# Strip sums S1, S2 and S4 in two PSUM banks with the products reordered, and the remainder of S3 made on GpSimd behind that of A12

## What is computed

```
def half_swiglu(x, g, w_up, w_down):
    h = rms_norm(x, g)
    a, b = jnp.split(h @ w_up, 2, axis=-1)
    return x + 0.5 * ((jax.nn.silu(a) * b) @ w_down)
```

## Time and profile before

| what | value |
|---|---|
| median of 3 runs | 2734.58 us (2734.44 to 2734.65) |
| span of the profiled execution | 2732.7 us |
| around its span, against the median of the runs | 1.9 us |
| PE busy | 2707.3 us, 99% |
| DVE busy | 1729.2 us, 63% |
| ACT busy | 1103.5 us, 40% |
| POOL busy | 999.8 us, 37% |
| mean granted TensorE clock | 0.998 |

### The profile page before, as it was taken

The page is one execution under the profiler, slowest core; times in us unless marked ns, Lnnn a source line. Parts: engine busy times, 40 slices in busy tenths (PEclk is TensorE's granted clock), DMA queues, the critical chain, the costliest instruction groups (busy, mean ns, idle before and its releaser), DMA issues. The chain is left out here.

```text
span 2732.7 us, 46951 instructions
## 1 busy us (share of the span) xinstructions
PE 2707.3 (99%) x18804; PEld 2646.4 (97%) x18804; DVE 1729.2 (63%) x2801; ACT 1103.5 (40%) x1858; POOL 999.8 (37%) x610
## 2 busy tenths in 40 slices
PE   9999999999999999999999999999999999999998
PEld 8999999998999999999999999999989999999997
DVE  8747576887433693838685647668773347837475
ACT  5324244636322352424443333454463224424242
POOL 2333333345433333333333333333544333333332
PEclk9999999999999999999999999999999999999999
DMA  3222222233122222222222222222332222222222
GB/s 118 99 71 93 77 87 93 88 124 125 63 71 91 75 73 84 78 93 78 94 77 85 70 95 78 92 86 88 132 109 70 77 88 74 75 79 78 93 78 85
DMA packets 72853, 238.04 MB, mean 87 GB/s; under 512 B 8304, under 2 KB 17264, under 8 KB 72176
## 3 DMA queue, kind: packets, MB, share of 16 engines
q1 hardware_dynamic: 57888, 208.30, 22.1%
q10 hardware_dynamic: 14800, 27.51, 2.9%
HBM read 227.52 MB, written 8.27 MB: 86 GB/s over the span
## 5 line engine op out<-in xcount | busy, mean ns | idle before, releaser
L498 POOL TENSOR_TENSOR w_lo<-w_raw,w_hi 128x1024 fp32r<-128x1024 f32 (+1 forms) x254 | 600.0, 2365 | 962.8 <-ACT w_hi L1131 947.7
L1131 ACT ACTIVATE w_hi<-w_raw 128x1024 fp32r<-128x1024 f32 (+1 forms) x238 | 250.2, 1051 | 796.1 <-PE lin L635 660.8
L635 PE MATMUL lin<-h_hi,w_hi 128*128 128x320 f32 x1600 | 373.8, 315 | 2.9 <-DVE tmp L1614 2.7
L635 PE MATMUL lin<-h_hi,w_lo 128*128 128x320 f32 x1600 | 364.6, 309 | 0.0
L635 PE MATMUL lin<-h_lo,w_hi 128*128 128x320 f32 x1600 | 364.1, 309 | 0.0
L635 PE MATMUL lin<-g_hi,w_lo 128*128 128x320 f32 x1408 | 320.9, 309 | 0.0
L635 PE MATMUL lin<-g_lo,w_hi 128*128 128x320 f32 x1408 | 320.8, 309 | 0.0
L635 PE MATMUL lin<-g_hi,w_hi 128*128 128x320 f32 x1408 | 320.7, 309 | 0.0
L550 POOL TENSOR_TENSOR lo_A<-raw_even,hi_A 128x512 fp32r<-128x512 f32 x120 | 167.8, 1398 | 376.3 <-ACT hi_A L1185 376.3
L635 PEld LDWEIGHTS lin<-h_hi,w_hi 128*128 128x128 f32 x1600 | 265.2, 188 | 15.9 <-issue 11.3
L635 PEld LDWEIGHTS lin<-h_lo,w_hi 128*128 128x128 f32 x1600 | 267.5, 188 | 0.0
(11 more groups left out here) (334 smaller groups left out, 6215.6 us busy)
## 6 DMA issues: line engine op xcount, KB each, us to landing
w_raw<-wts SPq DMA_DIRECT2D x240, 512.0 KB, 3.5
raw_even<-wts SPq DMA_DIRECT2D x88, 512.0 KB, 4.4
raw_odd<-wts SPq DMA_DIRECT2D x64, 512.0 KB, 4.2
caches<-kcache_in ACTq DMA_DIRECT2D x16, 512.0 KB, 4.0
caches<-vcache_in ACTq DMA_DIRECT2D x16, 512.0 KB, 4.7
x<-x_in SPq DMA_DIRECT2D x8, 320.0 KB, 6.6
k_out<-kT ACTq DMA_DIRECT2D x2, 1280.0 KB, 4.6
v_out<-v_sb ACTq DMA_DIRECT2D x2, 1280.0 KB, 8.6
```

Of the source, the lines that this page charges most:

```text
L498: ins = nc.gpsimd.tensor_tensor(w_lo[:, s, cols], w_raw[:, s, cols], w_hi[:, s, cols].bitcast(F), ALU.subtract)
L635: ins = nc.tensor.matmul(out[:, half, :], w, a[:, half * HALF:(half + 1) * HALF], start=first and n == 0, stop=last and n == 2)
L1131: nc.scalar.activation(w_hi[:, s, 0:cols], w_raw[:, s, 0:cols], ACT.Copy).then_inc(hi_ready.sem, 1)
```

## The change

Three things. (1) The sums S1, S2 and S4 of every pair but the first of a segment are made in place, one over the other, in a PSUM bank (`chain[i % 2]`, the two banks of `lin[1]`, which the linear tiles use outside the segments); pair 0 keeps SBUF strips. (2) M5(i) goes right behind M1(i), and the lists of ACT and DVE are written anew to fit. (3) The remainder of S3 is made by POOL, behind that of A12, for all pairs but the first of a segment.

```
+        chain = [lin[1][:, 0, :], lin[1][:, 1, :]]
...
@@ POOL, ffn
                             low_strip(L, q + i + 1, i + 1, "A12")
+                            low_strip(L, q + i + 1, i + 1, "S3")
...
@@ PE, segment
                         pe.wait_ge(evacuated.sem, evacuated.count(L, m))
+                    m5(L, q + i, i)
                     m6(L, q + i, i)
...
                     m7(L, q + i, i)
-                    m5(L, q + i, i)
                 m4(L, q + e, e)
...
@@ ACT, first_pair
                 hi_strip(L, q + 1, 1, "A11", "M1")
-                hi_strip(L, q + 1, 1, "S2", "M6")
+                hi_strip(L, q + 1, 1, "S1", "M5")
                 act.wait_ge(evacuated.sem, evacuated.count(L, m))
                 nc.scalar.activation(last_a[:, :], last_a[:, :], ACT.Silu).then_inc(silu_done.sem, 1)
                 hi_strip(L, q + 1, 1, "A12", "M2")
+                hi_strip(L, q + 1, 1, "S2", "M6")
                 hi_strip(L, q + 1, 1, "S3", "M7")
-                hi_strip(L, q + 1, 1, "S1", "M5")
...
@@ ACT, segment
                         hi_strip(L, q + i + 1, i + 1, "A11", "M1")
+                        hi_strip(L, q + i + 1, i + 1, "S1", "M5")
+                    if not i:
+                        hi_strip(L, q, 0, "A22")
+                        hi_strip(L, q, 0, "S4")
+                    if more:
+                        hi_strip(L, q + i + 1, i + 1, "S2", "M6")
                     if i:
+                        hi_strip(L, q + i, i, "A22", "M4")
+                        hi_strip(L, q + i, i, "S4", "M3")
                         silus(L, q + i - 1, i - 1)
                     if more:
                         hi_strip(L, q + i + 1, i + 1, "A12", "M2")
-                        hi_strip(L, q + i + 1, i + 1, "S3", "M7")
                     else:
                         act.wait_ge(product_done["M6"].sem, product_done["M6"].count(L, q + i + 1))
                         split(L, n)
                     if i:
                         keep_g(L, q + i - 1, slot0 + i - 1)
                     if more:
-                        hi_strip(L, q + i + 1, i + 1, "S1", "M5")
+                        hi_strip(L, q + i + 1, i + 1, "S3", "M7")
...
@@ DVE, add_strips
+                    if i >= 2:
+                        dve.wait_ge(strip_ready["S4"].sem, strip_ready["S4"].count(L, q - 1))
+                    elif i:
+                        dve.wait_ge(evacuated.sem, evacuated.count(L, m))
...
+                elif name == "S2" and i:
+                    dve.wait_ge(strip_ready["S1"].sem, strip_ready["S1"].count(L, q + 1))
+                    out, a, b, op = link, link, raw_[:, 0, :], ALU.subtract
...
@@ DVE, first_pair
                 keep_u2(L, q, 0)
-                add_strips(L, q + 1, 1, "S1")
+                add_strips(L, q + 1, 1, "S1", m)
+                add_strips(L, q + 1, 1, "S3")
+                lo_strip(L, q + 1, 1, "S1")
                 add_strips(L, q + 1, 1, "S2")
-                add_strips(L, q + 1, 1, "S3")
-                lo_strip(L, q + 1, 1, "S2")
                 lo_sums(L, f, "T4")
...
                 keep_u3(L, q, 0)
                 c22(L, q, 0)
                 lo_tokens(L, f, 2)
+                lo_strip(L, q + 1, 1, "S2")
                 add_strips(L, q + 1, 1, "S4")
-                lo_strip(L, q + 1, 1, "S3")
                 keep_u2(L, q + 1, 1)
```

More of the change, by code:

```diff
@@ L546, in low_strip @@
             def low_strip(L, q, i, name):
-                block_ = {"A11": 0, "A12": 1, "A22": 3}[name]
+                block_ = {"A11": 0, "A12": 1, "S3": 2, "A22": 3}[name]
                 pool.wait_ge(strip_hi_done[name].sem, strip_hi_done[name].count(L, q + 1))
@@ L1260, in segment @@
                         hi_strip(L, q + i + 1, i + 1, "A11", "M1")
[L1261 to L1264, removed]
+                        hi_strip(L, q + i + 1, i + 1, "S1", "M5")
+                    if not i:
+                        hi_strip(L, q, 0, "A22")
+                        hi_strip(L, q, 0, "S4")
+                    if more:
+                        hi_strip(L, q + i + 1, i + 1, "S2", "M6")
                     if i:
+                        hi_strip(L, q + i, i, "A22", "M4")
+                        hi_strip(L, q + i, i, "S4", "M3")
                         silus(L, q + i - 1, i - 1)
-                    if g == 0 and i == 1:
-                        hi_strip(L, q + 2, 2, "S2", "M6")
                     if more:
                         hi_strip(L, q + i + 1, i + 1, "A12", "M2")
-                        hi_strip(L, q + i + 1, i + 1, "S3", "M7")
                     else:
@@ L1689, in closing, with add_strips @@
                 reciprocal_root(L, p)
-            def add_strips(L, q, i, name):
+            def add_strips(L, q, i, name, m=None):
                 raw_ = raw_pair[i % 2]
+                link = chain[i % 2]
                 if name == "S1":
                     sem, count = pairs_landed(L, q)
-                    if q:
+                    if i >= 2:
+                        dve.wait_ge(strip_ready["S4"].sem, strip_ready["S4"].count(L, q - 1))
+                    elif i:
+                        dve.wait_ge(evacuated.sem, evacuated.count(L, m))
+                    elif q:
                         dve.wait_ge(strip_ready["S1"].sem, strip_ready["S1"].count(L, q))
                     dve.wait_ge(sem, count)
-                    out, a, b, op = S1_sum[:, :], raw_[:, 2, :], raw_[:, 3, :], ALU.add
+                    out, a, b, op = link if i else S1_sum[:, :], raw_[:, 2, :], raw_[:, 3, :], ALU.add
+                elif name == "S2" and i:
+                    dve.wait_ge(strip_ready["S1"].sem, strip_ready["S1"].count(L, q + 1))
+                    out, a, b, op = link, link, raw_[:, 0, :], ALU.subtract
                 elif name == "S2":
@@ L1832, in segment @@
                     more = i < e
[L1833 to L1838, removed]
+                    head = g == 0 and i == 1
+                    if i and not head:
+                        keep_u3(L, q + i - 1, i - 1)
                         c22(L, q + i - 1, i - 1)
-                        lo_strip(L, q + i, i, "S1")
+                    if not i:
+                        add_strips(L, q, 0, "S4")
                     if more:
-                        add_strips(L, q + i + 1, i + 1, "S1")
+                        add_strips(L, q + i + 1, i + 1, "S1", m)
+                        add_strips(L, q + i + 1, i + 1, "S3")
+                        lo_strip(L, q + i + 1, i + 1, "S1")
                         add_strips(L, q + i + 1, i + 1, "S2")
-                    if g or i > 1:
+                    if not head:
                         keep_u2(L, q + i, i)
                     if more:
-                        add_strips(L, q + i + 1, i + 1, "S3")
                         lo_strip(L, q + i + 1, i + 1, "S2")
-                    if i and (g or i > 1):
+                    if i:
                         c21(L, q + i - 1, i - 1)
-                    elif i == 0:
-                        add_strips(L, q, 0, "S4")
+                    else:
+                        lo_strip(L, q, 0, "S4")
+                    if head:
+                        lo_last(L, f)
                     if more:
                         add_strips(L, q + i + 1, i + 1, "S4")
-                    if i and (g or i > 1):
+                    if i:
                         c12(L, q + i - 1, i - 1)
-                    lo_strip(L, q + i, i, "S4")
-                    if i:
+                        lo_strip(L, q + i, i, "S4")
                         gate(L, q + i - 1)
[L1860 to L1863, removed]
                         lo_g(L, q + i - 1, slot0 + i - 1)
+                keep_u3(L, q + e, e)
                 c22(L, q + e, e)
@@ L1936, in ffn @@
                 for g in range(len(GROUPS)):
-                    segment(L, f, g, q, n0)
+                    segment(L, f, g, q, n0, m0)
                     q += SEGMENTS[g]
```

42 lines of the change are left out of this document (25 added, 17 removed).

## The result

The changed kernel took 2808.0 us (median of 4 runs, 2807.3 to 2808.8), the kernel before 2734.5 us beside it: ratio 1.027 (95% interval 1.0255 to 1.0284), 73.5 us slower. The forecast was 2791, the range 2770 to 2806. The profiled execution took 2808.6 us, with a span of 2806.8.

The account below looks back on a forecast made before the run. PE's matmul stream was taken to bound the kernel (busy 2707.3 of 2732.7 us). Ends 31.8, starts 8.1 and segments 0 17.2 sum to 57.1 us: span 2789.8, with 1.9 around it 2791.7, stated as 2791; range 2770 to 2806.

Parts of the forecast that it names:

- four groups of waits: PE waiting for u3 at 12 ends, u2 at 8 starts, S2's remainder and Silu 4 times each in segments 0.
- steady pairs: Pairs in the middle of segments: no new PE waits, price 0, with some 2 us of slack left.
- Ends: At 12 segment ends M4(e) waits for u3, behind a remainder of g blocked by POOL: 2.65 us each, 31.8 us.
- Starts: In 8 segments with g > 0, M7(0) waits for u2(0) behind the remainder of S1(1): 1.0 us each, 8.1 us.
- Segments 0: Segment 0 of each of the 4 FFNs: late first pairs cost 4.3 us each, 17.2 us.
- M6(1): In segment 0 it waits for the remainder of S2(1), now later in DVE's list: 1.7 us late, 5.1 in the first FFN.
- M1(2): In segment 0 it waits for pair 0's Silu, held by c12 and `lo_last` behind pair 2's sums: 2.6 us late.
- The sum of the waits: Over the whole kernel: 31.8 + 8.1 + 17.2 = 57.1 us added to the span of 2732.7.
- rival 3: Clock falls in new idle times: two products at half clock behind each end, 12 x 3.5 us more, 2833; chance 0.04.
- some of a slower clock: Part of the range's upper end, 2806, beside the case of the 8 starts also being blocked (10 us).
- PSUM at price 0: DVE writing sums to PSUM, in no row: taken as 0.68 us for 512 columns, as reading costs nothing more.
- all of it lies beside PE: In steady pairs, DVE's lost remainder to POOL and lower contention change nothing for PE: price 0.

Follow-up runs that it names:

- e1: Changed kernel with one DVE step moved: u3 of a segment's last pair ahead of the remainder of g of the pair before; 2775.0 us.
- e2: Changed kernel with one more wait on POOL: the first linear tile's remainder waits for DVE's remainder of g of the pair before the last; 2774.5 us.
- e5: Changed kernel with u2 of pair 0 ahead of the remainder of S1(1) on DVE, in the eight segments with g > 0; 2804.3 us.
- e3: Changed kernel with twelve matmuls, result not read, on PE ahead of M4(e) at the ends, dependencies kept; 2795.4 us.
- e8: e7 with the two PSUM banks of the chain replaced by two SBUF strips, all lists as in e7; 2759.0 us.
- e7: Changed kernel with the edits of e4, e5 and e6 together; PSUM banks, POOL's S3 and M5 behind M1 (all pairs but the last) stay; 2740.7 us.
- e6: Changed kernel with segment 0's lists reordered: on DVE S2(1)'s remainder, c21, `lo_last`, c12 earlier; on ACT pair 0's Silu earlier; 2790.2 us.
- e10: e7 with one more DVE step moved: u3 of pair 1 in segment 0 ahead of the remainder of S2 of pair 2; 2740.5 us.
- e12: Kernel before, order and lists unchanged, with S2 and S4 of all pairs but a segment's first in the two PSUM banks; 2732.0 us.
- e9: Changed kernel with twelve matmuls, result not read, ahead of the first product of the four segments with g = 2; 2817.5 us.
- e4: e1 with M5 of a segment's last pair alone put back behind M7 on PE; 2763.4 us.

## Why the prediction was right and wrong

- **Direction, places, causes: right.** All four groups of waits came where and as often as foretold, and none in the steady pairs.
- **Ends: right.** 2.65 foretold, 2.50 measured, 12 of 12. Both parts, the order and the port, were taken away singly (e1, e2), and each time the wait fell to what u3 is worth by itself.
- **Starts: right.** 1.0 foretold, 0.94 measured, and e5 removed them.
- **Segments 0: nearly right.** M6(1) 1.7 foretold and 1.42 measured (5.1 and 4.9 in the first FFN); M1(2) 2.6 and 2.50, but only 1.6 in the first FFN. 17.2 foretold net of the old waits, 15.3 measured.
- **The sum of the waits**: 57.1 us net foretold, 52.8 measured (55.8 less 3.0). By itself that would have been 2787, 4 us under the forecast and inside the range. The rest up to 2808 is the 1.4 us at the start of the execution and the 19.9 us behind the waits.
- **The step that failed is rival 3, the clock.** It was given 0.04 and left out of the sum, on the ground that in the earlier trace rows the clock was still 1.00 in a stretch of 3.20 us without work. The rows were read as a bound, "no less than that lets it fall"; they show one case. The runs put in its place: in the changed kernel 11 of 15 waits with 2.34 us of idle PE were followed by a half-rate stretch, and e3 removed those behind the ends by keeping PE busy. Each costs 1.3 to 1.5 us, some 17 in all, and they, not the waits, are why the time came out above the forecast. Even the very wait of the earlier trace rows, 3.13 us at the program's end, has no fixed point at which the clock falls: before, it was 1.00 to the end of the wait; in e3's trace it is at 0.50 from 1.36 us into it:

```profile
2780.01:2781.36 1.35, 0.00 (x1) 0.00 (x0) 0.90 (x2) 0.34 (x1) 0.00 (x0) 1.00 0.00 0
2781.36:2783.14 1.78, 0.00 (x0) 0.00 (x0) 1.55 (x4) 0.00 (x0) 0.00 (x0) 0.50 0.00 0
```

Also wrong was that rival's price: all ends at 3.5 us each, 42 us, instead of most of the long waits at 1.3 to 1.5. The range's upper end held only "some of a slower clock", and missed by 2 us.

- **PSUM at price 0** was right for what the forecast compared, but "all of it lies beside PE" holds only for the steady pairs: e8 shows that without it the openings and first pairs would lose 18 us more with e7's lists.
- Of e6, e7 and e10 the sum was 6 to 9 us off, because each took the removed wait as won. The next late steps in the lists took part of it back: in e7 and e10 the segments 0 are still 5.7 us longer than before. In what order the openings would be free of waits stays open.

## What to carry to other kernels

When a product is moved in a packed stream, look at the ends and starts of the loop first: the steady round can be perfect while the last product loses the neighbour that covered its wait. Price a wait of an otherwise saturated PE with its clock: here 2.3 us of idle cost up to 1.5 us more behind it in most places, and filling the wait with matmuls whose result nobody reads got that back. Time freed on an engine pays only where something waits for it: 50 us less work on DVE gave 2.4 us with the old lists (e12), and the new lists, made to use it, took 6 us more than the kernel before even when mended (e7), though without it they would have taken 24 (e8).

## What was not expected of the hardware

The granted clock halved behind a wait of 2.34 us with PE idle, in some places and not in others, for the same wait in the same surroundings: behind 8 of 12 ends in the trace of the changed kernel, behind 10 in that of e6, 11 in that of e9 and all 12 in that of e5. In the segments the half-rate stretches were 3.41 us long; behind the wait of 4.7 us there was one of 6.83 us in three traces (the changed kernel, e1, e4) and of 3.41 in four (e2, e3, e5, e9). The segments' waits of 1.26 to 2.00 us had none behind them, one of 2.06 us (e9) had, and of the four of 3.0 us in e8 one had none. DVE wrote its sums to PSUM at the speed of SBUF: 0.70 us for 512 columns, against 0.69 in the earlier trace rows, with PE writing other banks at the same time.
